# Eight weight groups prepared before the first tile: four staging buffers in turn, the low halves on VectorE alone

## The chip, the cores and the metric

The kernel runs on one core of a Trainium2 chip. The metric is the device time of one execution in microseconds (us), the median of three runs. The core has a matrix engine (TensorE, PE in the profile), VectorE (DVE), ScalarE (ACT), GpSimd (POOL), and queues that start transfers (SyncE, SP, here). Each engine works through its own list of instructions in order, and the engines wait for each other by semaphores that are written out by hand.

## The reference

One layer of a hybrid decoder over a prompt of 2048 tokens and 8 single new tokens, model width 1024, in fp32. What matters here:

```
u = rmsnorm(x, norm_in)
proj = u @ w_in                      # 1024 x 2832, split into nine parts
z = g_low @ w_gate_up + b_gate;  log_a = log_sigmoid(z) / 16
o_gla = gated linear attention(gq, gk, gv, log_a)       # 4 heads, recurrent state
o_swa = sliding-window attention(sq, sk, sv, sinks)     # 8 heads, window 128
h = x + concat(rmsnorm(o_gla) * silu(g_gate), o_swa * silu(s_gate)) @ w_out
y = rmsnorm(h, norm_f)
```

## The kernel before

Every product of an activation with a weight is made of fp16 matmuls: both factors are split into a high and a low half, and three matmuls (high by high, high by low, low by high) are added up in one PSUM bank. So the weights have to be split before anything can be multiplied by them, and they have to be scaled first so that the largest fits fp16.

**Preparing the weights.** The weights come in eight groups (`PREP`): group 0 is `sklow` (272 columns), 1 `gqk`, 2 `sq`, 3 `gv`, 4 `gg`, 5 `sg`, 6 and 7 the halves of the output projection (512 columns each). A group is 8 row blocks of 128 rows. For group i:

- `load_w(i)` (SP) brings it as fp32 into a staging buffer. There are four: two halves of the scratch tensor `flex`, and the room of `w_out_hi` and of `w_out_lo`, which are not in use yet. A buffer is loaded again when the group in it has been split.
- `sum_w(i)` (ACT) and `row_bound(i)` (DVE) bound the values in it, ACT over the last row blocks by summing, DVE over the first `SUM_ROWS` by a maximum. `row_bound` ends with a column `w_col`.
- `bound(i)` (PE) sums that column over the partitions with a matmul by ones (line 548), and `scale_w(i)` (DVE) makes the scale of it.
- `hi_w(i)` (ACT, line 1052, 8 instructions) writes the high half; `lo_w(i)` writes the low half, source times scale minus high half: DVE (line 1502) for row blocks 2 to 7, POOL (lines 1822 and 1825) for row blocks 0 and 1.

DVE's order in group i is: first half of `lo_w(i)`, `scale_w(i + 1)`, second half of `lo_w(i)`, `row_bound(i + 2)`. ACT's order is `hi_w(i)`, `sum_w(i + 2)`.

**Tiles.** The prompt is worked through in 16 tiles of 128 tokens, then the 8 new tokens. The projections of a tile (`proj`, units `sklow`, `gqk`, `sq`, `gv`, `gg`, `sg`) are made on PE one tile ahead, so that PE has work while the other engines do the attention of the current tile; those of tiles 0 and 1 lie beside the preparation. A unit of 512 columns is 24 matmuls of 512 columns, or 96 of 128. The results of the units pass through two PSUM banks in turn (`pj`, a `Ring`): the third unit from any unit waits until ACT or DVE has taken the first out (`take_qk`, `take_sq`, `take_gate` on ACT, `take_kv`, `take_gv` on DVE). Its list for the first tiles is bc0, sklow0, bc1, gqk0, sklow1, gqk1, sq0, sq1, gv0, gv1, gg0, sg0, gg1, sg1, where the digit is the tile.

**A tile.** In `body(t)` DVE takes the gate logits z (`take_z`), the maxima of the first two score banks (`row_max`) and the running sums of the decays (`sums`), then multiplies the transposed probabilities by a window mask (`take_pt`, line 1378), builds the factors of the linear attention (`factors`), assembles its scores, and ends with norms, scaling and residual. PE follows: `values` (line 611), `leaf_scores` (line 637), `level_scores` (line 651), `gla_out` (lines 671 and 675), `turn_out` (line 698), `out_proj`. Most of what a tile works on lies in `flex`, so in the room of two staging buffers.

## Time and profile before

| | us |
|---|---|
| median of 3 runs | 1002.18 (1001.75 to 1004.89) |
| the profiled execution | 1003.19 |
| its span, first to last instruction | 1001.0 |
| preparation and the middle of tile 0 | 0 to 119.4 |
| tile 0 ends on PE | 149.8 |
| one tile afterwards | 54.0 |
| last tile and the 8 new tokens | from about 930 |

PE is busy for 924.5 us (92% of the span), DVE for 665.4, ACT for 377.6, POOL for 100.9. The table is read so: from 119.4 us on PE goes from one piece of work to the next, tile after tile; the idle time of PE lies ahead of that and at the end.

### The profile page before, as it was taken

The page shows a single profiled execution, that of the slowest core. Times are in us where ns is not written, and L with a number is a line of the kernel's source. Part 1 is how long each engine was busy: PE and PEld are TensorE (multiplying, and loading weights), DVE is VectorE, ACT ScalarE, POOL GpSimd, SP SyncE. Part 2 cuts the span into 40 slices and gives each one's busy share as a digit, 9 for nine tenths or more (in the row PEclk, how much of TensorE's full clock was granted, in tenths as well). Part 3 has the DMA queues.
Part 4 walks back from the last instruction along what each step waited for, and adds up shares of the span by engine and source line. Part 5 has one row for each costly group of instructions (what it writes and reads, how often), then busy time and mean ns, then how long its engine had stood idle before and what let it go on. Part 6 is the DMA issues. An engine that isn't in the chain of part 4 may idle for free.

```text
span 1001.0 us, 22336 instructions
## 1 busy us (share of the span) xinstructions
PE 924.5 (92%) x8445; PEld 658.1 (66%) x8445; DVE 665.4 (66%) x1953; ACT 377.6 (38%) x1016; POOL 100.9 (10%) x125
## 2 busy tenths in 40 slices
PE   1598599999999999999999999999999999999977
PEld 1573458686767757585768666675758586866855
DVE  5888858575675748485757657574858585765573
ACT  4774434343324333333434232433333343424210
POOL 1453301010100101010101000010101010101000
PEclk9799599999999999999999999999999999998776
DMA  8621102020202001020202020110102020101220
GB/s 328 269 107 64 63 1 86 1 86 1 87 1 75 12 26 62 2 85 2 87 1 85 2 87 1 45 42 18 70 1 86 1 86 1 46 1 44 77 105 23
DMA packets 15238, 56.77 MB, mean 57 GB/s; under 512 B 3569, under 2 KB 5001, under 8 KB 13840
## 3 DMA queue, kind: packets, MB, share of 16 engines
q1 hardware_dynamic: 14832, 55.09, 14.8%
q8 instruction: 79, 1.29, 0.5%
q14 instruction: 39, 0.32, 0.1%
q10 hardware_dynamic: 288, 0.07, 0.0%
HBM read 44.36 MB, written 10.78 MB: 55 GB/s over the span
## 4 chain that ended last, share of the span: by engine, by line
PE 85%; DVE 12%; issue 2%; DMA 1%; ACT 0%; DVEq 0%; SPq 0%
PE bank L508 21%; PE bank L510 21%; PE bank L509 21%; PE bank L611 6%; PE bank L651 3%; DVE w_in_hi_lo L1502 2%; DVE w_abs L1472 2%; PE bank L588 2%; PE bank L698 2%; PE bank L600 1%; PE bank L675 1%; PE bank L671 1%; DVE flex L1378 1%; PE bank L625 1%; PE bank L637 1%
## 5 line engine op out<-in xcount | busy, mean ns | idle before, releaser
L508 PE MATMUL bank<-u_hi,w_in_hi_lo 128*128 128x128 f16 (+1 forms) x1288 | 210.1, 215 | 11.3 <-DVE w_in_hi_lo L1502 11.3
L510 PE MATMUL bank<-u_hi,w_in_hi_lo 128*128 128x128 f16 (+1 forms) x1288 | 209.9, 215 | 5.4 <-issue 5.4
L509 PE MATMUL bank<-u_lo,w_in_hi_lo 128*128 128x128 f16 (+1 forms) x1288 | 209.9, 215 | 0.0
L508 PE MATMUL bank<-w_in_hi_lo,u_hi 128*128 128x512 f16 (+3 forms) x528 | 177.8, 344 | 0.8 <-ACT win_q L951 0.5
L510 PE MATMUL bank<-w_in_hi_lo,u_lo 128*128 128x512 f16 (+3 forms) x528 | 177.6, 344 | 0.0
L509 PE MATMUL bank<-w_in_hi_lo,u_hi 128*128 128x512 f16 (+3 forms) x528 | 177.6, 344 | 0.0
L508 PEld LDWEIGHTS bank<-u_hi,w_in_hi_lo 128*128 128x128 f16 x1288 | 125.5, 100 | 24.3 <-DVE w_in_hi_lo L1502 11.4
L509 PEld LDWEIGHTS bank<-u_lo,w_in_hi_lo 128*128 128x128 f16 x1288 | 124.5, 99 | 0.1
L510 PEld LDWEIGHTS bank<-u_hi,w_in_hi_lo 128*128 128x128 f16 x1288 | 124.6, 99 | 0.0
L508 PE MATMUL bank<-w_out_hi,ogT_hi 128*128 128x512 f16 x256 | 98.0, 383 | 0.0
L509 PE MATMUL bank<-w_out_lo,ogT_hi 128*128 128x512 f16 x256 | 97.9, 382 | 0.0
L510 PE MATMUL bank<-w_out_hi,ogT_lo 128*128 128x512 f16 x256 | 97.8, 382 | 0.0
L611 PE MATMUL bank<-win_v,flex 128*128 128x64 f32 x512 | 69.8, 288 | 19.2 <-DVE flex L1378 19.2
L611 PEld LDWEIGHTS bank<-win_v,flex 128*128 128x128 f32 x512 | 67.5, 206 | 27.7 <-DVE flex L1378 23.6
L510 PEld LDWEIGHTS bank<-w_in_hi_lo,u_lo 128*128 128x128 f16 (+1 forms) x528 | 52.4, 99 | 46.7 <-issue 0.7
L508 PEld LDWEIGHTS bank<-w_in_hi_lo,u_hi 128*128 128x128 f16 (+1 forms) x528 | 52.4, 99 | 45.0 <-issue 4.8
L509 PEld LDWEIGHTS bank<-w_in_hi_lo,u_hi 128*128 128x128 f16 (+1 forms) x528 | 52.4, 99 | 39.6 <-issue 0.8
L1833 POOL TENSOR_TENSOR flex<-decay_sum_leaf 128x256 f32<-128x256 f32 x16 | 11.5, 718 | 594.4 <-DVE decay_sum_leaf L1273 594.4
L1226 DVE TENSOR_TENSOR xT<-xT,bank 128x1024 f32<-128x1024 f32 (+1 forms) x17 | 19.7, 1161 | 77.4 <-PE bank L518 77.4
L991 ACT ACTIVATE flex<-flex,win_stat 128x128 f32<-128x128 f32 x128 | 50.4, 394 | 31.4 <-DVE win_stat L1367 31.2
L1019 ACT CAST ogT_hi<-bank 128x512 f16<-128x512 f32 x32 | 17.3, 588 | 92.5 <-PE bank L698 92.5
L510 PEld LDWEIGHTS bank<-w_out_hi,ogT_lo 128*128 128x128 f16 x256 | 25.3, 99 | 30.8 <-issue 1.1
(252 smaller groups left out, 1636.9 us busy)
## 6 DMA issues: line engine op xcount, KB each, us to landing
xT<-in_xT SPq DMA_DIRECT2D x16, 512.0 KB, 4.5
x_rows<-in_xq SPq DMA_DIRECT2D x16, 512.0 KB
flex<-in_w SPq DMA_DIRECT2D x4, 2048.0 KB, 9.1
flex<-in_xq SPq DMA_DIRECT2D x16, 512.0 KB, 3.3
out_y<-flex SPq DMA_DIRECT2D x16, 512.0 KB, 2.6
w_out_hi<-in_w SPq DMA_DIRECT2D x2, 2048.0 KB, 8.6
w_out_lo<-in_w SPq DMA_DIRECT2D x1, 2048.0 KB, 14.6
flex<-in_w SPq DMA_DIRECT2D x1, 1088.0 KB, 7.4
```

Of the source, the lines that this page charges most:

```text
L508: nc.tensor.matmul(out, a_hi, b_hi, start=start and i == 0, stop=False)
L509: nc.tensor.matmul(out, a_hi, b_lo, start=False, stop=False)
L510: mm = nc.tensor.matmul(out, a_lo, b_hi, start=False, stop=stop and i == last)
L588: mm = nc.tensor.matmul(at_ring.bank(name, t)[:, i * 2 * P:(i + 1) * 2 * P], sq[r:r + HD, t.p, 2 * pair + i, :], kwin[r:r + HD, t.p, :], s ...
L611: mm = nc.tensor.matmul(accS[:, c:c + HD], PT[:, u % 2, i, kb, :], vwin[:, t.p, kb, h * HD:h * HD + HD], start=kb == 0, stop=kb == 1)
L651: mm = nc.tensor.matmul(bank[:, c:c + P], EX[:, l0 + l, f, :], QE[:, l0 + l, f].rearrange("p h c -> p (h c)"), start=True, stop=True)
L698: tp = nc.tensor.transpose(bank[:, k * P:k * P + n], gates[0:n, c:c + P], ident[0:n, 0:n])
L991: e = nc.scalar.activation(PR[:, u % 2, i, :], PR[:, u % 2, i, :], ACT.Exp, scale=-1.0, bias=wst[:, 0, k:k + 1], accum_out=wst[:, 1, k:k + 1])
L1019: nc.scalar.copy(ogT_hi[:, 4 * g:4 * g + 4, 0:n], bank[:, :, 0:n]).then_inc(act_o.sem, 1)
L1226: V.tensor_tensor(xT[:, :, 0:n], xT[:, :, 0:n], bcast(pj.bank("bc", t)[:, 0:n], 1, DT), ALU.mult).then_inc(pj.freed["dve"], 1)
L1472: V.tensor_reduce(wabs[:, s, 0:SUM_ROWS], staged(i)[:, 0:SUM_ROWS], AX.X, ALU.max, apply_absolute_value=True).then_inc(w_dve, 1)
L1502: lo = V.scalar_tensor_tensor(out=w_slice(PREP[i], w_lo, wo_lo)[:, d], in0=staged(i)[:, d], scalar=gs[:, i % 2, d:d + 1], in1=w_slice(PREP ...
```

## The change

Four things are changed, all of them ahead of tile 1; the loop over the later tiles and the ending keep their instructions.

- **Staging in turn.** Groups go to the four buffers in turn, beginning with `w_out_hi` and `w_out_lo`. SP starts groups 0, 1 and 2 at once, then the second tile's x, then group 3, the constants, and groups 4 to 7 in order.
- **GpSimd leaves the weights.** DVE makes all eight row blocks of the low half.
- **ScalarE sums four row blocks instead of three**, squares instead of absolute values, and DVE's maximum covers four instead of five. The bound is now a root of a sum of squares, rounded to a power of two by integer arithmetic on the exponent: `row_bound` has two more small instructions, `scale_w` works without a reciprocal.
- **Preparation first.** Before, tile 0's z, maxima and sums were taken ahead of the last group. Now they come after it. On PE the `bound` matmuls stand in other places between the projections, `gg` and `sg` of tile 0 are projected before the tile's work, and 18 of the 24 matmuls of tile 1's `gg` stand around `leaf_scores`.

```diff
-STAGE_OF = [0, 1, 2, 3, 0, 2, 1, 0]
-LOAD_ORDER = [0, 1, 2, 3, 4, 6, 5, 7]
-POOL_ROWS = 2
-SUM_ROWS = 5
+STAGE_OF = [2, 3, 1, 0, 2, 3, 1, 0]
+SUM_ROWS = 4
...
             load_w(1)
+            load_w(2)
             load_x(Tile(1))
-            for i in LOAD_ORDER[2:4]:
-                load_w(i)
+            load_w(3)
...
@@ PE, ahead of the tiles @@
             proj(Tile(1), "gqk")
+            proj(Tile(0), "sq")
             bound(4)
-            proj(Tile(0), "sq")
             proj(Tile(1), "sq")
+            proj(Tile(0), "gv")
             bound(5)
-            proj(Tile(0), "gv")
+            proj(Tile(1), "gv")
+            pe.wait_ge(init, 1)
+            turn_low(Tile(0))
             bound(6)
-            proj(Tile(1), "gv")
+            proj(Tile(0), "gg")
             bound(7)
-            pe.wait_ge(init, 1)
+            proj(Tile(0), "sg")
...
@@ PE, in body(t), where early is tile 0 @@
                 turn_probs(t, 3)
+                if early:
+                    proj(nxt, "gg", 3)
                 leaf_scores(t)
-                if not early:
+                if early:
+                    proj_rest(nxt, "gg", 3, 6)
+                else:
                     proj(nxt, "gv")
...
@@ ACT, sum_w @@
                 for d in range(SUM_ROWS, DT):
-                    a = nc.scalar.activation(unread[d - SUM_ROWS], src[:, d], ACT.Abs,
+                    a = nc.scalar.activation(unread[d - SUM_ROWS], src[:, d], ACT.Square,
                                              accum_out=wabs[:, i % 2, d:d + 1])
...
@@ ACT, body(t) @@
+                log_gate(t)
+                probs(t, 0)
+                probs(t, 1)
+                if early:
+                    act.wait_ge(w_lo_done, NG)
+                    take_gate(t, 0)
+                    take_gate(t, 1)
+                    nc.scalar.preload_act_table_set(LOG_EXP_SET)
+                else:
                     take_sq(nxt)
                 decays(t)
...
@@ DVE, row_bound and scale_w @@
+                V.scalar_tensor_tensor(out=wsq[:, s, 0:m], in0=wabs[:, s, 0:m], scalar=float(n), in1=wabs[:, s, 0:m],
+                                       op0=ALU.mult, op1=ALU.mult)
+                V.tensor_tensor(wsq[:, s, m:DT], wabs[:, s, m:DT], w_gain(PREP[i])[:, m:DT], ALU.mult
+                                ).then_inc(w_dve, 1)
...
-                V.reciprocal(wcol[:, 3:4], wcol[:, 2:3]).then_inc(w_dve, 1)
+                V.tensor_scalar(scale, half_exp, -EXP_ONE, 189 * EXP_ONE, ALU.mult, ALU.add)
+                V.tensor_scalar(unscale, half_exp, EXP_ONE, 65 * EXP_ONE, ALU.mult, ALU.add).then_inc(w_dve, 1)
...
@@ DVE, lo_w @@
-                for d in (range(POOL_ROWS, 4), range(4, DT))[half]:
+                for d in (range(4), range(4, DT))[half]:
...
@@ POOL @@
-            for i in range(NG - 1):
-                lo_w(i)
-            differences(Tile(0))
-            lo_w(NG - 1)
```

The order of the instructions shows two places on which the prediction speaks. First PE between the second `gqk` (128-column matmuls) and the second `gv` (512 columns). The rows with `w_col,ones` are `bound(4)` and `bound(5)`; of each projection only the first matmul stands, with its waits (`proj_freed_act`: until ACT has taken a result out of the bank). Before:

```order
L548 MATMUL bank<-w_col,ones 128x1 [waits w_row_bound_done]
L508 MATMUL bank<-u_hi,w_in_hi_lo 128x128 [waits proj_freed_dve,dve_norm,w_lo_pool,w_lo_done]
...
L508 MATMUL bank<-u_hi,w_in_hi_lo 128x128 [waits proj_freed_act,dve_norm,w_lo_pool,w_lo_done]
...
L548 MATMUL bank<-w_col,ones 128x1 [waits w_row_bound_done]
L508 MATMUL bank<-w_in_hi_lo,u_hi 128x512 [waits proj_freed_act,dve_norm,w_lo_pool,w_lo_done]
```

And of the changed kernel, from `sq` of tile 0 on:

```order
L504 MATMUL bank<-u_hi,w_in_hi_lo 128x128 [waits dve_norm,proj_freed_dve,w_lo_done]
...
L544 MATMUL bank<-w_col,ones 128x1 [waits w_row_bound_done]
L504 MATMUL bank<-u_hi,w_in_hi_lo 128x128 [waits dve_norm,proj_freed_act,w_lo_done]
...
L504 MATMUL bank<-w_in_hi_lo,u_hi 128x512 [waits dve_norm,proj_freed_act,w_lo_done]
...
L544 MATMUL bank<-w_col,ones 128x1 [waits w_row_bound_done]
L504 MATMUL bank<-w_in_hi_lo,u_hi 128x512 [waits dve_norm,proj_freed_act,w_lo_done]
```

`bound(4)` moved behind `sq` of tile 0, and `bound(5)` behind `gv` of tile 0, whose first matmul waits for a bank that ACT frees.

Second SP at the start. Before (`w_out_hi` here holds group 2, `w_out_lo` group 3):

```order
L438 DMA flex<-in_w 128x2176
L438 DMA flex<-in_w 128x4096
L422 DMA xT<-in_xT 128x1024
L427 DMA x_rows<-in_xq 128x1024
L438 DMA w_out_hi<-in_w 128x4096
L438 DMA w_out_lo<-in_w 128x4096
```

and in the changed kernel, where the first `flex` holds group 2 and the second group 3:

```order
L435 DMA w_out_hi<-in_w 128x2176
L435 DMA w_out_lo<-in_w 128x4096
L435 DMA flex<-in_w 128x4096
L420 DMA xT<-in_xT 128x1024
L425 DMA x_rows<-in_xq 128x1024
L435 DMA flex<-in_w 128x4096
```

Group 2 moved ahead of the second tile's x, whose load waits until the first tile's is used up.

## Rows read from the trace of the kernel before

**Rows 1.** The page: TensorE's granted clock in 40 slices of the span.

```profile
PEclk9799599999999999999999999999999999998776
```

**Rows 2.** Windows by stage: length, busy time (count) by engine, PEclk, DMA share, GB/s.

```profile
core 0: us, PE busy (x) PEld busy (x) DVE busy (x) ACT busy (x) POOL busy (x), PEclk, DMA share, GB/s
0.00:141.00 141.00, 90.59 (x769) 67.12 (x769) 111.34 (x232) 79.80 (x180) 47.06 (x34) 0.87 0.38 148
203.80:930.00 726.20, 713.97 (x6498) 502.46 (x6495) 475.18 (x1485) 265.22 (x748) 48.79 (x83) 1.00 0.11 39
```

**Rows 3.** Waits of PE, 0 to 130 us: total, times, longest.

```profile
PE bank L548 <- DVE w_col L1478: 16.3, 6, 4.4
PE bank L611 <- DVE flex L1378: 12.3, 2, 9.6
```

**Rows 4.** Timeline, SP and ACT: start, duration, what, idle before and its releaser.

```profile
15.33 0.43 SPq L438 DMA_DIRECT2D w_out_hi<-in_w  x1
15.81 3.39 ACT L1052 ACTIVATE w_in_hi_lo<-flex,w_scale 128x272 f16<-128x272 f32 x8
25.34 0.63 ACT L1040 ACTIVATE junk<-w_out_hi 128x512 bf16<-128x512 f32 x1 [5.11 <-DMA w_out_hi<-in_w]
48.85 5.01 ACT L1052 ACTIVATE w_in_hi_lo<-w_out_lo,w_scale 128x512 f16<-128x512 f32 x8
67.97 1.25 ACT L951 ACTIVATE win_q<-bank,inv_scale_q 128x512 f32<-128x512 f32 x2
```

**Rows 5.** Timeline, DVE and POOL where both work on a group.

```profile
54.70 2.13 POOL L1825 TENSOR_TENSOR w_in_hi_lo<-w_out_lo,w_in_hi_lo 128x1024 f16<-128x1024 f32 x1
54.88 1.97 DVE L1476 TENSOR_TENSOR w_abs<-w_abs,norm_in 128x8 f32<-128x8 f32 x1
63.87 3.65 POOL L1822 TENSOR_SCALAR flex<-flex,w_scale 128x512 f32<-128x512 f32 x2 [7.04 <-ACT w_in_hi_lo L1052]
64.69 1.40 DVE L1502 SCALAR_TENSOR_TENSOR w_in_hi_lo<-flex,w_scale,w_in_hi_lo 128x512 f16<-128x512 f32 x2
```

**Rows 6.** Timeline, DVE: the steps of a group, and marks in tile 0.

```profile
28.43 2.81 DVE L1472 TENSOR_REDUCE w_abs<-w_out_hi 128x5 f32<-128x2560 f32 x1
39.77 1.22 DVE L1232 TENSOR_TENSOR u_lo<-xT,u_hi 128x1024 f16<-128x1024 f32 x1
58.29 0.15 DVE L1485 TENSOR_SCALAR w_col<-bank 128x1 f32<-128x1 f32 x1
58.81 2.73 DVE L1502 SCALAR_TENSOR_TENSOR w_in_hi_lo<-w_out_lo,w_scale,w_in_hi_lo 128x512 f16<-128x512 f32 x4
61.46 2.81 DVE L1472 TENSOR_REDUCE w_abs<-w_out_hi 128x5 f32<-128x2560 f32 x1
86.92 0.15 DVE L1485 TENSOR_SCALAR w_col<-bank 128x1 f32<-128x1 f32 x1
94.80 0.61 DVE L1258 TENSOR_SCALAR flex<-bank,b_gate 128x128 f32<-128x128 f32 x2 [2.09 <-PE bank L625]
102.30 6.95 DVE L1502 SCALAR_TENSOR_TENSOR w_out_lo<-flex,w_scale,w_out_hi 128x512 f16<-128x512 f32 x6
110.36 1.22 DVE L1378 TENSOR_TENSOR flex<-bank,window_mask 128x512 f32<-128x512 f32 x2
134.90 0.88 DVE L1431 TENSOR_SCALAR flex<-flex,row_max 128x512 f32<-128x512 f32 x2
```

**Rows 7.** Windows at the edges of PE's pieces, columns as in the second group.

```profile
39.91:56.38 16.47, 16.47 (x242) 16.29 (x242) 16.28 (x24) 10.03 (x20) 10.99 (x6) 0.84 0.60 224
57.34:68.23 10.89, 10.89 (x196) 10.89 (x195) 8.65 (x15) 9.58 (x23) 4.28 (x3) 1.00 0.05 21
68.89:74.23 5.34, 5.34 (x24) 2.25 (x24) 5.34 (x6) 4.76 (x9) 2.62 (x3) 1.00 0.20 46
85.94:92.96 7.02, 7.02 (x26) 2.75 (x26) 6.74 (x11) 1.19 (x3) 4.82 (x3) 0.76 0.00 0
119.41:125.54 6.13, 6.13 (x35) 6.05 (x36) 2.66 (x10) 4.04 (x5) 1.04 (x1) 0.64 0.00 1
125.54:129.23 3.69, 3.69 (x23) 2.56 (x23) 2.58 (x7) 1.42 (x3) 0.00 (x0) 1.00 0.02 4
129.23:149.80 20.57, 20.57 (x108) 10.24 (x108) 10.22 (x27) 7.81 (x19) 0.00 (x0) 1.00 0.00 0
```

More of the change, by code:

```diff
@@ L436, in load_w @@
                     sp.wait_ge(w_lo_done, before[-1] + 1)
-                    sp.wait_ge(w_lo_pool, before[-1] + 1)
                 sp.dma_start(staged(i).rearrange("p d c -> p (d c)"), w_d[:, off:off + DT * n]
@@ L452, in _ @@
                 sp.dma_start(dst, src).then_inc(const_in, 16)
-            for i in LOAD_ORDER[4:]:
+            for i in range(4, NG):
                 load_w(i)
             sp.wait_ge(w_lo_done, NG)
-            sp.wait_ge(w_lo_pool, NG)
             sp.wait_ge(w_hi_done, 2 * NG)
@@ L807, in _ @@
             proj(Tile(0), "sklow")
+            bound(2)
             bc(Tile(1))
-            bound(2)
             proj(Tile(0), "gqk")
@@ L826, in body @@
                 early = t.static and t.off == 0
-                turn_low(t)
-                if early:
-                    proj(t, "gg")
-                    scores(t, 0)
-                    gate_up(t)
-                else:
-                    proj(nxt, "gqk")
-                    gate_up(t)
-                    scores(t, 0)
-                if early:
-                    proj(t, "sg")
-                else:
+                if not early:
+                    turn_low(t)
+                    proj(nxt, "gqk")
+                gate_up(t)
+                scores(t, 0)
+                if not early:
                     proj(nxt, "sq")
@@ L856, in body @@
                 turn_keys(t)
-                proj(nxt, "gg", 3)
+                if early:
+                    proj_rest(nxt, "gg", 6)
+                else:
+                    proj(nxt, "gg", 3)
                 gla_out(t)
                 state_update(t)
-                proj_rest(nxt, "gg", 3)
+                if not early:
+                    proj_rest(nxt, "gg", 3)
                 proj(nxt, "sg", 5)
@@ L1484, in scale_w @@
                 dve.wait_ge(w_bound, i + 1)
[L1485 removed]
+                half_exp, unscale, scale = (wcol[:, k:k + 1].bitcast(I32) for k in (1, 2, 3))
+                V.tensor_scalar(half_exp, accG[:, i:i + 1].bitcast(I32), 24, None, ALU.logical_shift_right
                                 ).then_inc(w_dve, 1)
[L1487 to L1489 removed]
+                dve.wait_ge(w_dve, 5 * i + 4)
+                V.tensor_scalar(scale, half_exp, -EXP_ONE, 189 * EXP_ONE, ALU.mult, ALU.add)
+                V.tensor_scalar(unscale, half_exp, EXP_ONE, 65 * EXP_ONE, ALU.mult, ALU.add).then_inc(w_dve, 1)
+                dve.wait_ge(w_dve, 5 * i + 5)
+                V.tensor_scalar(gs[:, i % 2, :], w_gain(g), wcol[:, 3:4], W_TOP, ALU.mult, ALU.mult
+                                ).then_inc(w_scaled, 1)
+                c = 1.0 / W_TOP / (U_SCALE if g < len(GROUPS) else 1.0)
                 V.tensor_scalar(inv[:, g:g + 1], wcol[:, 2:3], c, None, ALU.mult)
@@ L1676, in _ @@
             V.memset(ones[:, :], 1.0).then_inc(ones_set, 1)
+            V.memset(kwin[:, 0, 0:P], 0.0)
+            V.memset(vwin[:, 0, 0, :], 0.0)
+            V.memset(S_bd[:, :, :, :], 0.0)
             dve.wait_ge(first_in, 16 * 2)
@@ L1685, in _ @@
             for i in range(NG):
-                if i == NG - 1:
-                    dve.wait_ge(w_lo_done, i)
-                    dve.wait_ge(w_lo_pool, i)
-                    take_z(Tile(0))
-                    row_max(Tile(0), 0)
-                    row_max(Tile(0), 1)
-                    sums(Tile(0))
                 lo_w(i, 0)
@@ L1708, in _ @@
                     scale_u(Tile(1))
-                if i == 1:
+                if i == 3:
                     dve.wait_ge(const_in, 16 * 13)
                     V.tensor_scalar(s_sink[:, 1:2], s_sink[:, 0:1], -1.0, None, ALU.mult)
-                    V.tensor_scalar(nsink[:, :], sink[:, :], -1.0, None, ALU.mult)
-                    V.memset(kwin[:, 0, 0:P], 0.0)
-                    V.memset(vwin[:, 0, 0, :], 0.0)
-                    V.memset(S_bd[:, :, :, :], 0.0).then_inc(init, 1)
+                    V.tensor_scalar(nsink[:, :], sink[:, :], -1.0, None, ALU.mult).then_inc(init, 1)
+                if i == 4:
+                    take_gv(Tile(0))
                 if i == 5:
-                    take_gv(Tile(0))
-                if i == 6:
                     take_gv(Tile(1))
             dve.wait_ge(w_lo_done, NG)
-            dve.wait_ge(w_lo_pool, NG)
             V.memset(QE, 0.0).then_inc(init, 1)
@@ L1726, in body @@
                 early = t.static and t.off == 0
-                if not early:
-                    take_z(t)
-                    row_max(t, 0)
-                    row_max(t, 1)
-                    sums(t)
+                take_z(t)
+                row_max(t, 0)
+                row_max(t, 1)
+                sums(t)
                 take_pt(t, 0)
@@ L1815, in _ @@
             G = nc.gpsimd
-            def lo_w(i):
-                pool.wait_ge(w_hi_done, 2 * i + 1)
-                src = staged(i)
-                for d in range(POOL_ROWS):
-                    s = G.tensor_scalar(src[:, d], src[:, d], gs[:, i % 2, d:d + 1], None, ALU.mult)
-                s.then_inc(w_in_place, 1)
-                pool.wait_ge(w_in_place, i + 1)
-                G.tensor_tensor(w_slice(PREP[i], w_lo, wo_lo)[:, 0:POOL_ROWS], src[:, 0:POOL_ROWS],
-                                w_slice(PREP[i], w_hi, wo_hi)[:, 0:POOL_ROWS], ALU.subtract).then_inc(w_lo_pool, 1)
             def differences(t):
@@ L1844, in gates_over_sums @@
                 G.tensor_tensor(g, g, bcast(wst[:, 5, :], 2, HD), ALU.mult).then_inc(pool_w.sem, 1)
-            for i in range(NG - 1):
-                lo_w(i)
-            differences(Tile(0))
-            lo_w(NG - 1)
             def body(t):
-                if not (t.static and t.off == 0):
-                    differences(t)
+                differences(t)
                 gates_over_sums(t)
```

63 lines of the change are left out of this document (19 added, 44 removed).

## The prediction, made before the changed kernel had run

> **What bounds the kernel now.** I began with the page's clock row and the windows by stage. The clock is full in nearly every slice but the first five and the last four [rows 1]. In the stage from 203.8 to 930 us PE is busy for 713.97 of 726.20 us, DVE for 475.18 [rows 2]: the loop over the tiles is bound by PE. The change leaves its instructions alone, so it can move only the ramp, 0 to 141 us, where PE is busy for 90.59 us and DVE for 111.34. PE's waits there say for what: 16.3 us for `w_col`, and 12.3 us for the masked probabilities of tile 0, one of them 9.6 us [rows 3]. Both are DVE's. From 119.41 us, when `values` of heads 4 to 7 begins, PE is busy to the edge of every window [rows 7]. The question is when PE gets to that point, and how much work is left behind it.
>
> **The price of a group on DVE.** A bundle of four low-half instructions goes from 58.81 to 61.46, 2.65 us [rows 6]; two more per group cost 1.32. The maximum over five blocks takes 2.81 us [rows 6]; four blocks cost between 4/5 of it (2.25) and all of it; a part of an instruction is fixed, so I take 2.28, 0.53 saved. Two more small instructions in `row_bound`, and one independent one in `scale_w`: each lies between nothing and 0.2, by `scale_w`'s own, four of them in 58.81 - 58.29 = 0.52 [rows 6]. I take 0.28 and 0.10. Against that the stalls beside POOL go: POOL's TENSOR_TENSOR runs from 54.70 to 56.83, and DVE's 8-element instruction, begun inside it, needs 1.97 us, where its neighbours take some 0.2 [rows 5]: about 1.9 us a group. So 1.32 - 0.53 + 0.38 - 1.9, a gain of 0.7 us a group, 5 to 6 over the eight. A group now costs DVE 2.87 (`row_bound`) + 0.62 (`scale_w`) + 5.30 (`lo_w`) = 8.8 us.
>
> POOL's other form is not in that sum: DVE's two low-half instructions at 64.69 took their usual 1.40 us though POOL's TENSOR_SCALAR ran from 63.87 to 67.52 [rows 5]. [...]
>
> **The start.** Group 2 was issued at 15.33 and ACT waited 5.11 us for it, until 25.34 [rows 4]; the norm of tile 1's x stands behind it on ACT, and DVE's maximum of group 2 began at 28.43 [rows 6]. Now group 2 is issued with the first two. ACT does four sums of 0.62 instead of three, so `hi_w(0)` ends near 15.81 + 0.61 + 3.3 = 19.7 [rows 4]. Before, 1 MB of x and then its 2 MB came within 10.0 us; at that rate the 6 MB of x, groups 0, 1 and 2 are there near 20, and less late with no gap in between: I take 19; at worst it lands when it did. ACT then sums until 22.2, squares x until 23.4, and after 0.7 us of statistics and 0.8 on DVE the maximum begins at 24.8: 3.6 us earlier. From it, `row_bound` 2.87, `take_kv` 0.66 at 27.9 (it waits for `sklow`), the x product 1.2 behind `bc`, now queued behind `bound(2)`, to 29.9, then 2.65 + 0.67 + 2.65: `lo_w(1)` ends at 35.9 instead of 39.77 [rows 6], 3.9 us earlier.
>
> **Where it goes.** PE is next. `gqk` of tile 0, `sklow` and `gqk` of tile 1 took 16.47 us from that point, partly at half clock (0.84 on the mean) [rows 7]. PE still idles for some 7 us ahead of it, so I keep the 16.47: 36.0 to 52.5. `sq` of tile 0 (half of 10.89 [rows 7]) now stands ahead of `bound(4)`: 57.9. DVE, ready for `scale_w(4)` at 53.7, gets it at 58.2. Before it got it at 58.29 [rows 6]. The 3.9 us are gone, though PE has one unit more behind it.
>
> The next step is worse. `bound(5)` stands behind `gv` of tile 0, which needs the bank of `sq0`; ACT frees it after `hi_w(4)` and `sum_w(6)`. So 58.2 + 0.7 (`scale_w(4)` up to its signal), + 4.9 (`hi_w`, [rows 4]) + 2.46 (four sums) + 0.63 (half of 1.25, [rows 4]): `gv0` begins at 66.9. It takes 5.34 us at full clock [rows 7]; before, `gv1`, 24 matmuls behind an idle stretch of 3.9 us, took 7.02 at a mean clock of 0.76 [rows 7]. Here PE idles 3.5 us (`sq1` ends at 63.5). Ends 5.34 and 7.02, with 7.8 if the half clock held as long as it did behind 39.91; nearest is 7.02. So `scale_w(5)` is at 74.2 (72.5 at full clock), while DVE stood ready at 67. I count a new stall of 5 to 7 us in DVE.
>
> From there nothing else is late: two groups with a `take_gv` each, 2 x (8.8 + 0.66) = 18.9; then from `scale_w(7)` 0.62 + 3 x 2.65 and 1.1 for the wait and memset ahead of tile 0: `take_z` at 102.8. Before, from 86.92 (`scale_w(7)`) to 110.36 (`take_pt`) it took 23.44 us, with z, maxima and sums (94.80 to 102.30, 7.5 us) inside and 6.95 for the last six low-half instructions [rows 6]. Now 9.7 + 7.5 = 17.2: `take_pt` at 110.3 instead of 110.36. The same time. Moving z behind the last group costs nothing by itself, since DVE does the same work in either order; ACT's two gates and table loads (3.9 us) fit beside `sums` and `take_pt`, with 0.5 us to spare before `factors`.
>
> **Behind `take_pt`.** 18 matmuls of `gg1`, once behind `turn_keys`, now stand around `leaf_scores`. Before, `values` began 9.05 us behind `take_pt` (119.41 - 110.36) and PE had idled. Now PE has `values` of heads 0 to 3, two transposes (to +5.1), nine matmuls at half clock (0.427 each, 3.8), `leaf_scores` 1.1, nine more at full clock 1.95 (3.8 at half): +12 to +14. Then the levels 3.9 us at full clock instead of 6.13 [rows 7], six matmuls 1.3 and `gla_out` 1.9: +19.1. Before `gla_out` ended at 129.23, +18.9. A draw. From there PE had 20.57 us [rows 7]; 15 matmuls (3.2 us) of that are gone, but `turn_out` needs the scaled rows, half of them at 134.90 + 0.44, 6.1 us behind `gla_out` [rows 6]. So only the slack goes: PE would reach it at +3.8 and waits until +6.2, saving 20.57 - 19.9 = 0.7 us.
>
> **Sum.** `take_pt` -0.1, `gla_out` +0.2, end -0.7 and a rounding of the last terms: -0.8 us. Against the profiled execution (1003.19, of which 1001.0 is span) that is 1002.4; against the median, 1002.18, it is 1001.4. I predict 1001.4.
>
> **Rivals.**
> *A, the clock stays up* (chance 0.20). Ahead of `gv0` the idle stretch is a little shorter than the 3.9 us after which the clock fell; in full clock `gv0` ends 1.7 us earlier, and if `gqk0` warms up one matmul unit sooner another 1 to 2 us come. -2.5 to -5, median near 998.6. For it: the 0.7 us gaps in rows 7 cost no clock. Against: 3.5 is near 3.9.
> *B, DVE bound throughout* (0.03). Without either `bound` wait DVE would be at `scale_w(5)` at 61, 13 us earlier: 988. Against it: PE alone needs 36.0 + 16.47 + 10.89 + 5.34 = 68.7 to get there.
> *C, PE is cold where it was warm: slower* (0.13). The mechanism is the new idle stretch ahead of `turn_out`, 2.4 us, behind `gla_out`. If it drops the clock, the last `sg` matmuls and the output projection run up to 5 us at half speed, 2.5 us lost; with the second nine of `gg1` cold (1.9) and `gv0` at 7.8 (0.8) it gives -0.8 + 5.2 = +4.4, 1006.6. It decides from the length of idle at which the clock falls: the 3.9 us ahead of 85.08 were enough, 0.7 us ahead of 68.89 were not [rows 7].
> *D, x1 behind group 2* (0.07). If x of tile 1 lands late or group 2 lands at 25, the 3.6 us of the start are lost. `gqk0` starts at 39.6, everything follows: +2.8, 1005.0.
> Forecast: 0.57.
>
> A measurement of this kernel can tell about 0.3%, 3 us, from no change. Faster by more: most of A's upper half and B, and a tail of the forecast, 0.20. Slower: C and part of D, 0.14. Same 0.66. The range reaches from A's middle to the near side of C: 998 to 1005.5.
>
> **What would show it.** In the profile of the changed kernel: DVE's small instructions at some 0.2 us everywhere; no ACT wait for group 2; DVE's maximum of group 2 near 24.8 and `gqk0` near 36; `bound(4)` near 58 and DVE idle 4 us ahead of it; PE waiting for `win_q` ahead of `gv`, DVE idle for 5 us or more ahead of `scale_w(5)` near 73; `take_pt` near 110; a PE wait of 2 us ahead of `turn_out`; tile 0 ending near 149. I am wrong if `gv0` doesn't wait, if the granted clock in it or in the output projection of tile 0 is other than said, or if a later tile takes longer than before (726.2 us for the stage [rows 2], 54.0 each).

## The result, and the profile after

| | before | changed |
|---|---|---|
| median, us | 1003.08 (1001.75 to 1004.89, 6 runs) | 1008.21 (1007.05 to 1013.38, 6 runs) |
| ratio to before, 95% | | 1.0066 (1.0049 to 1.0083) |
| span of the profiled execution | 1001.0 | 1005.8 |
| first mark: first `values` of tile 1 | 164.48 | 164.38 |
| from there to the first `values` of tile 14 | 707.24 | 712.36 |
| the rest | 129.28 | 129.06 |

The changed kernel is 5 us slower. The prediction said 1001.4 (998.0 to 1005.5). The lower three rows split the span at two marks: the first matmuls of `values` in tile 1, where the loop over the tiles has just begun, and those in tile 14, the second tile behind the loop. The ramp came out the same, as forecast, but that the two marks lie within 0.1 us of each other is luck: in the kernels below whose ramp is that of the changed kernel the first mark lies between 162.4 and 164.7, and in those with the ramp of the kernel before between 162.9 and 164.5. The whole loss lies in the loop, which the forecast took as fixed.

Of the executions behind the numbers below, one of the kernel before (1583.92 us) and one of `after_pad128` (1211.95 us, at a mean granted clock of 0.741) were in a slow state; the ratios leave both out, and so does the median given for `after_pad128`.

**The ramp.** The windows by stage of the changed kernel, columns as in [rows 2]:

```profile
0.00:141.00 141.00, 93.27 (x769) 64.82 (x770) 106.06 (x272) 85.66 (x196) 3.74 (x10) 0.87 0.38 148
203.80:930.00 726.20, 712.24 (x6470) 503.07 (x6467) 472.05 (x1471) 263.30 (x739) 48.84 (x83) 0.99 0.11 39
```

VectorE has 5.3 us less to do in the ramp, GpSimd next to nothing. The timeline of ACT and DVE in the changed kernel, at the places forecast (start, duration, what, idle before and its releaser):

```profile
19.79 0.61 ACT L1039 ACTIVATE ogT_hi<-flex 128x512 bf16<-128x512 f32 x1
24.85 2.28 DVE L1462 TENSOR_REDUCE w_abs<-flex 128x4 f32<-128x2048 f32 x1
57.23 0.16 DVE L1480 TENSOR_SCALAR w_col<-bank 128x1 int32<-128x1 int32 x1 [4.21 <-PE bank L544]
73.25 0.16 DVE L1480 TENSOR_SCALAR w_col<-bank 128x1 int32<-128x1 int32 x1 [7.02 <-PE bank L544]
101.96 0.48 DVE L1248 TENSOR_SCALAR flex<-bank,b_gate 128x128 f32<-128x128 f32 x2
109.33 1.28 DVE L1368 TENSOR_TENSOR flex<-bank,window_mask 128x512 f32<-128x512 f32 x2
```

ACT no longer waits for group 2 (5.11 us in [rows 4]), and VectorE's maximum of it begins at 24.85 instead of 28.43 [rows 6]. Then both gains go where the prediction saw them go: VectorE idles 4.21 us for `bound(4)` and 7.02 us for `bound(5)`, and `take_pt` is at 109.33 instead of 110.36. Windows of the changed kernel at `gv` of tile 0, at the last nine `sg` matmuls of tile 0's pass, and from `gla_out` to the end of the tile:

```profile
66.07:73.10 7.03, 7.03 (x27) 3.04 (x28) 0.16 (x1) 0.47 (x1) 0.00 (x0) 0.76 0.13 54
135.34:139.12 3.78, 3.78 (x12) 1.40 (x10) 1.96 (x6) 3.11 (x6) 0.00 (x0) 0.55 0.00 0
128.12:149.70 21.58, 19.21 (x93) 9.11 (x93) 10.22 (x27) 7.93 (x19) 0.00 (x0) 0.92 0.00 0
```

`gv0` ran at a mean clock of 0.76 and took 7.03 us. Behind the new idle stretch ahead of `turn_out` (2.37 us) the clock was down for eight or nine matmuls: the window took 3.78 us at a mean clock of 0.55, so some 1.7 us more than the 2.1 (3.78 x 0.55) that it takes warm, at full clock. That is the first term of rival C, which had it at 2.5 us; its two others did not come (the second nine `gg` matmuls ran at full clock, 1.00 from 118.30 to 123.00 us, and `gv0` took 7.03 us and not 7.8).

**The loop.** Rows of PE's and DVE's waits from 150 to 910 us (total, times, longest), before:

```profile
PE bank L611 <- DVE flex L1378: 6.9, 14, 0.5
PE bank L510 <- issue: 5.4, 5, 1.2
```

and in the changed kernel:

```profile
PE bank L606 <- DVE flex L1368: 10.8, 14, 1.6
DVE flex L1251 <- issue: 3.8, 3, 1.4
PE bank L506 <- issue: 3.3, 5, 0.9
DVE flex L1251 <- DVE flex L1248: 1.7, 2, 0.9
```

The second and fourth rows are new. L1248 and L1251 are the two steps of `take_z`, and no work stands between them in the program. "issue" means that the engine waited for nothing that the profile shows. The loop makes six passes of two tiles each, and so jumps back from the end of its body to its first instruction, its head, five times. Five times, once for each jump, VectorE stood still in `take_z`. The place behind the first jump, before (VectorE's timeline):

```profile
265.03 0.61 DVE L1258 TENSOR_SCALAR flex<-bank,b_gate 128x128 f32<-128x128 f32 x2 [2.92 <-PE bank L625]
265.67 0.29 DVE L1261 TENSOR_SCALAR flex<-flex 128x256 f32<-128x256 f32 x1
```

and in the changed kernel, with PE's row of `values` that waits at the end of it:

```profile
264.34 0.61 DVE L1248 TENSOR_SCALAR flex<-bank,b_gate 128x128 f32<-128x128 f32 x2 [2.32 <-PE bank L620]
266.36 0.29 DVE L1251 TENSOR_SCALAR flex<-flex 128x256 f32<-128x256 f32 x1 [1.41 <-issue]
273.96 2.32 PE L606 MATMUL bank<-win_v,flex 128*128 128x64 f32 x15 [1.62 <-DVE flex L1368]
```

PE's idle 1.62 us there was 0.53 before, and it has a price of its own. The next windows, before and changed:

```profile
273.56:278.00 4.44, 4.44 (x61) 4.44 (x62) 4.33 (x21) 2.77 (x9) 0.00 (x0) 1.00 0.02 4
```

```profile
273.96:278.00 4.04, 4.04 (x33) 4.04 (x34) 3.94 (x20) 2.76 (x9) 0.00 (x0) 0.66 0.00 0
```

The granted clock was 0.66 on the mean here, and it fell again behind the last jump, at 713 us (0.77 over 4 us). Each of these two tiles took 55.47 us from its `values` to those of the next tile instead of 53.84. So the 5.12 us are: PE's waits for the probabilities +3.9 (10.8 - 6.9), cold matmuls, at half clock (0.50 from 275.30 to 278.60 us and from 715.60 to 718.90), +3.3 (2 x 1.63), PE's own idle behind the jump -2.1 (3.3 - 5.4). That sums to 5.1.

**What VectorE waits for.** The list of DMA queues has two rows of instruction packets (packets, MB, share). In the windows of 0.2 us in which they fall, q14 has one at 261.8, one at 264.4 and one at 268.6 in the changed kernel. The second:

```profile
q14 instruction: 1, 0.01, 18.0%
```

It is on its way when VectorE stops behind L1248, at 264.95. Its own time, 18.0% of 16 engines' 0.2 us, is 0.58 us, so it ends near 265.0, and VectorE goes on at 266.36, 1.3 us later; at the four other jumps it goes on 1.3 to 1.5 us behind the end of such a packet too. What fills that time no trace shows. A packet is 8 KB (0.32 MB in 39). This makes a fetch of VectorE's own instructions the suspect, and the experiments begin there. In the compiled programs VectorE's stream has 351 instructions in the loop, from number 295 before and from number 327 in the changed kernel: the rewritten ramp moved the loop by 32 instructions. PE's loop, 2014 long, begins at 1669 before and at 1657 after. The loops of ScalarE and GpSimd moved as well; the memsets of the experiments leave them where they are.

### The profile page after: what moved, and what is told of

It is laid out like the page before. It is cut to its first block, busy times and chain, and to the rows that moved or that the text cites. A ratio compares the mean times of both kernels' runs of the same rounds, so it can differ in the third digit from the quotient of the medians.

```text
span 1005.8 us, 22346 instructions
## 1 busy us (share of the span) xinstructions
PE 930.2 (92%) x8445; PEld 658.6 (65%) x8445; DVE 660.0 (66%) x1993; ACT 382.5 (38%) x1032; POOL 57.6 (6%) x101
## 4 chain that ended last, share of the span: by engine, by line
PE 85%; DVE 10%; issue 2%; ACT 1%; DMA 1%; SPq 0%; DVEq 0%
PE bank L504 21%; PE bank L506 21%; PE bank L505 21%; PE bank L606 6%; PE bank L646 3%; PE bank L693 2%; PE bank L583 2%; PE bank L595 1%; PE bank L670 1%; PE bank L666 1%; DMA w_out_lo<-in_w 1%; DVE w_in_hi_lo L1497 1%; PE bank L632 1%; DVE w_out_lo L1497 1%; PE bank L620 1%
## 5 line engine op out<-in xcount | busy, mean ns | idle before, releaser
L504 PE MATMUL bank<-w_in_hi_lo,u_hi 128*128 128x512 f16 (+3 forms) x528 | 180.0, 349 | 4.1 <-issue 4.1
L505 PE MATMUL bank<-w_in_hi_lo,u_hi 128*128 128x512 f16 (+3 forms) x528 | 179.5, 348 | 0.0
L996 ACT ACTIVATE win_stat<-win_stat 128x8 f32<-128x8 f32 x16 | 3.3, 208 | 110.7 <-DVE win_stat L1374 110.7
```

Of the source, the lines that this page charges most:

```text
L504: nc.tensor.matmul(out, a_hi, b_hi, start=start and i == 0, stop=False)
L505: nc.tensor.matmul(out, a_hi, b_lo, start=False, stop=False)
```

## The experiments

Each gives its own median, with that of the kernel before on the same chip in brackets. "Head" is the number of the first instruction of the loop in VectorE's stream. "Stall" adds up the idle time in `take_z` over the five jumps. "Loop" is the time from the first `values` of tile 1 to those of tile 14, in the profiled execution, and "first mark" is where it begins. With the loop, 39 or 40 packets on q14 mean five fetches for each jump (39 - 14 = 25 over five jumps); 14 or 15 mean none within the loop. Loop, stall and marks are those of one execution each.

| kernel | VectorE's head | q14 packets | stall in `take_z` | loop | first mark | median |
|---|---|---|---|---|---|---|
| before | 295 | 39 | 0 | 707.24 | 164.48 | 1003.08 |
| changed | 327 | 39 | 5.5 | 712.36 | 164.38 | 1008.21 |
| after_pad8 | 335 | 14 | 0 | 706.04 | 162.43 | 1001.91 (1003.88) |
| before_pad31 | 326 | 40 | 4.1 | 708.29 | 163.65 | 1006.30 (1003.88) |
| after_pad64 | 391 | 39 | 0 | 706.82 | 163.37 | 1002.66 (1003.25) |
| after_pad128 | 455 | 40 | 7.3 | 713.06 | 163.30 | 1007.92 (1003.25) |
| after_pad136 | 463 | 15 | 0 | 705.30 | 164.69 | 1002.12 (1003.05) |
| before_pad44 | 339 | 15 | 0 | 707.86 | 164.06 | 1002.81 (1003.05) |
| after_pad8_pe | 335 | 15 | 0 | 707.16 | 162.51 | 1003.08 (1003.17) |
| after_bounds | 327 | 39 | 3.7 | 710.47 | 156.00 | 998.41 (1003.88) |
| after_bounds_pad8 | 335 | 14 | 0 | 705.16 | 154.62 | 993.05 (1003.88) |
| after_flat | none | 29 | 0 | 700.73 | 163.84 | 996.71 (1003.25) |
| before_flat | none | 28 | 0 | 700.72 | 162.87 | 995.87 (1003.25) |
| bounds_flat | none | 29 | 0 | 700.72 | 154.62 | 987.34 (1003.05) |
| bounds_flat_gg | none | 29 | 0 | 700.70 | 160.11 | 992.20 (1003.05) |
| bounds_flat_gg9 | none | 29 | 0 | 700.71 | 154.79 | 987.68 (1003.17) |

### Moving VectorE's loop head

**after_pad8** and **before_pad31** put small instructions on VectorE ahead of everything, while it waits for the first transfers (before, its second instruction begins at 7.67 us; in `after_pad128` 60 of the memsets took 1.72 us). The tiles are untouched; `before_pad31` differs in 31 for 8 and starts from the kernel before.

```diff
             V.memset(ones[:, :], 1.0).then_inc(ones_set, 1)
+            for k in range(8):
+                V.memset(pad[:, k:k + 1], 0.0)
```

> The changed kernel with eight one-column memsets added at the start of VectorE's program, where VectorE is idle until 7.7 us. Nothing else changes, so the ramp should end where it does (tile 0 at 149.7 us). Theory F (instruction fetch behind the loop's back edge: the two instructions of take_z, L1248 and L1251, are torn apart by up to 1.4 us because a block of VectorE's program ends between them): moving the loop by eight instructions takes the edge of the block ahead of the loop's first instruction; the 'issue' idle time ahead of take_z's third instruction goes (3.8 us in 3 cases before), no stage of the loop has a clock under 1.00, and the time falls by 3 to 5 us, to 1003 to 1005. Rival P (the loop got slower since tile 0 leaves it in another state, by clock or by phase): the time stays at 1008.

> The kernel before, with 31 one-column memsets at the start of VectorE's program, where it is idle; by a count of rows and waits this sets its loop where that of the changed kernel stands. Theory F: the ramp is as before (tile 0 ends at 149.8 us), the idle time between take_z's instructions appears behind the back edges, and the kernel before gets slower by 2 to 5 us with no change of its work, to 1005 to 1008. If the count is off by a few instructions, the gap appears some instructions later, or not at all. Rival P: 1003 as before.

Eight idle instructions made the changed kernel 6 us faster by the medians: ratio to before 0.998 (0.9968 to 0.9991) instead of 1.0066. That is more than the 3 to 5 us expected. In the profiles the loop is 6.3 us shorter; the first mark comes 2.0 us earlier, since the clock stayed up in `gv0` (last section), and behind the loop 2.1 us are lost again. Its queue and wait rows:

```profile
q14 instruction: 14, 0.11, 0.0%
```

```profile
PE bank L607 <- DVE flex L1369: 6.9, 14, 0.5
PE bank L507 <- issue: 2.7, 5, 0.8
```

The fetches are gone, the stall is gone, and PE's wait is 6.9 us as before. In the other direction, 31 instructions brought the stall into the kernel before (ratio 1.0027, 1.0015 to 1.0039; median 1006.30, within the 1005 to 1008 expected):

```profile
PE bank L612 <- DVE flex L1379: 9.4, 14, 1.3
PE bank L511 <- issue: 3.8, 5, 0.9
DVE flex L1262 <- issue: 2.2, 2, 1.1
DVE flex L1262 <- DVE flex L1259: 1.9, 3, 0.8
```

Here the clock never fell in the loop, which lost 1.1 us: PE's waits for the probabilities +2.5 (9.4 - 6.9), its own idle behind the jump -1.6 (3.8 - 5.4). But the profiled execution was the fastest of ten. Seven of the others took 1005.6 to 1008.1 us, at mean granted clocks of 0.953 to 0.956, and the two others took 1003.3 and 1003.7, at 0.959 and 0.957; no trace shows where their clock was lost. So the same stall costs 1 to 5 us, and part of that is what the clock does with it. Why PE's own idle time fell here, with its head at 1669 as before, is not shown.

**after_pad64** and **after_pad128** ask whether it is the place or just some memsets: the same edit with 64 and 128.

> The changed kernel with 64 one-column memsets on VectorE near its beginning (59 ns each at most, while VectorE waits for the first transfers); the tiles are untouched. Measured from the first `values` after tile 0 to the last, the loop took 707.2 us before, 712.4 changed, 706.0 with 8 memsets, and its trace shows on queue q14, in packets of 8 KB (128 instructions of 64 bytes), 39 instruction packets before and changed, 14 with 8 memsets. Theory F (the place of the loop in VectorE's instruction stream decides, in blocks of 128): the loop, some 350 instructions long, lies over three blocks with 8 memsets and over four with 64. So q14 has some 39 packets again, but the loop's first block ends long behind take_z, as before, so that no stall stands between take_z's instructions: loop 706.5 to 708.5, median 1003 +-2. Rival G (extra instructions ahead of the loop shift the phase of the engines or of the clock, and any number of them helps): 14 packets or no relation, loop 706 as with 8. Rival H (blocks of 256, edge beyond +64): no fetches, 706.

The 64 bytes of an instruction can be estimated from the runs. The cost of the jump comes back after 128 memsets (below), and from none to 128, as from 8 to 136, q14 has one packet of 8 KB more (39 and 40, 14 and 15): 8192 / 128 = 64. A count of one packet is coarse, as 31 memsets brought one too. The other queue, q8, fits the same size. In `after_flat` it has 50 packets of 16 KB from 163.84 to 864.57 us, over thirteen tiles of 1007 instructions of PE (2014 / 2), or 62.6 bytes an instruction; 64 would be 51 packets:

```profile
q8 instruction: 50, 0.82, 0.5%
```

> As the last, with 128 memsets: one whole block. Theory F: the loop lies against the block edges just as in the changed kernel without memsets. q14 has 39 or 40 packets, VectorE stands for some 1.1 to 1.4 us between take_z's two forms behind back edges, loop 711 to 713, median 1008 +-2. Rival G: loop 706, median 1002. Rival H (blocks of 256): the edge is half a block away, no stall there, loop 706 to 708.

With 64 the fetches are back and hurt nobody in the profiled execution, which was the second fastest of ten; four of the others took 1004.5 to 1008.3 us, so the median's interval (ratio 1.0005, 0.9986 to 1.0025) leaves room for a small cost. With 128 everything is as with none, the stall larger still:

```profile
q14 instruction: 40, 0.33, 0.1%
```

```profile
PE bank L607 <- DVE flex L1369: 12.6, 14, 1.9
DVE flex L1252 <- issue: 7.3, 5, 1.7
PE bank L507 <- issue: 2.2, 5, 0.8
```

That rules out that any number of memsets helps, by the phase of the engines or of the clock (rival G), and blocks of 256 (rival H).

**after_pad136** and **before_pad44** are the cures one block further on, and for the kernel before.

> The changed kernel with 136 memsets, one block and 8. Theory F: as with 8, some 14 or 15 packets on q14 (one more block ahead of the loop), no stall in take_z, loop 706, median 1002 +-2. If more memsets only make things worse (128 gave 713): 712 or more, median 1008.

> The kernel before with 44 one-column memsets on VectorE near its beginning, which puts its loop where it lies in the changed kernel with some 4 to 13 memsets (the changed kernel has 40 instructions more ahead of the loop, or 31 with the separate waits counted). Theory F: the loop fits three blocks, q14 has some 14 instruction packets instead of 39, no fetch within the passes, loop from first to last `values` 706.0 instead of 707.2, median 1001.5 +-1.5. If memsets are no cure but only the changed kernel's ramp with 8 is: 39 packets and 707 to 708, as with 31 memsets.

`after_pad136` came out as said: 15 packets, 705.3 us. So heads 335 and 463 are free of fetches, 295, 326, 327, 391 and 455 are not: a period of 128, with an edge of a block between 327 and 335. A loop of 351 instructions that begins up to 33 behind an edge lies over three blocks (3 x 128 = 384), elsewhere over four; the packets fit three blocks that stay and four that don't. In `before_pad44` the fetches went too, but its loop stayed at 707.86: half of that expectation failed. VectorE had no stall to lose there, and what stands out in that loop is PE's own idle time behind the jump:

```profile
PE bank L511 <- issue: 5.5, 5, 1.2
```

**after_pad8_pe** moves PE's head instead, from 1657 to the 1669 of the kernel before.

```diff
                 pe.wait_ge(w_row, i + 1)
+                for k in range(3 if i == 0 else 0):
+                    nc.tensor.matmul(accG[:, i:i + 1], ones[:, :].broadcast_to([P, P]), wcol[:, 0:1],
+                                     start=True, stop=True)
```

> The changed kernel with the 8 memsets on VectorE, and on PE three more copies of the first `bound` matmul (each 4 instructions in the compiled program, the same value written again), so that PE's loop begins at instruction 1669 of its stream as in the kernel before, not at 1657. Theory F': what a back edge costs depends on where each engine's loop lies in its own stream; PE's idle time `<- issue` ahead of the first projection behind it was 5.4 us in all (5 times, longest 1.2) in both kernels with the head at 1669, whatever VectorE did, and 2.2 to 4.2 (longest 0.9) in those at 1657. So here 5 to 5.6, longest 1.2, no fetches of VectorE within the passes (14 packets), and a loop of 707.4 to 708.2, as the 707.9 of the kernel before with 44 memsets. Rival: PE's idle time there comes from other differences of the kernel before: 2.7, 706.0 as without the copies.

```profile
PE bank L507 <- issue: 4.9, 5, 1.2
```

PE's idle stretches of 1.2 us came back, behind three of the five jumps; the loop took 707.16 us, against 706.04 without the copies. That is in the direction of the expectation and a little short of it (707.4 to 708.2). Without a stall of VectorE's the loop took 705.16 to 706.82 us in the four profiles with PE's head at 1657, and 707.16 to 707.86 in the three with 1669. So PE's place seems to matter, by about 1 us over the loop, and the change then gained this microsecond, which hid a part of what VectorE lost. It is less certain than VectorE's part: each loop is one execution, the medians cannot show 1 us (ratios 0.998, 0.9968 to 0.9991, without the copies and 1.0001, 0.9986 to 1.0016, with them), and `before_pad31`, with its head at 1669, had 3.8 us of this idle time, longest 0.9.

### No loop at all

**after_flat** and **before_flat** write the twelve tiles of the loop out (the expectations speak of ten tiles in five passes; it is six passes and five jumps).

```diff
-            with eng.Fori(0, (NT - 4) // 2) as j:
-                body(Tile(1, j))
-                body(Tile(2, j))
-            for n in range(NT - 3, NT - 1):
+            for n in range(1, NT - 1):
                 body(Tile(n))
```

> The changed kernel without the loop: the ten tiles of its five passes are written out one behind the other, the same instructions in the same order on every engine. Theory F: nothing jumps back, the instructions come in order, and every tile takes the 53.84 us of the tiles without a back edge: from first to last `values` 13 x 53.84 = 699.9 us instead of 712.4, median near 1008.2 - 12.5 = 995.7 (994 to 998). Rival I (the later tiles are longer because the changed ramp leaves PE, the other engines or the clock in another phase, whatever the loop is): the loop keeps its 5 us on before's, 705 us, and after_flat is some 5 us slower than before_flat.

> The kernel before without the loop, in the same way. Theory F: 13 x 53.84 = 699.9 instead of 707.2, median near 1003 - 7.3 = 995.7 (994 to 998): the same as after_flat within 2 us, so that without the loop the change is worth about nothing, as its ramp shows. Rival I: 5 us less than after_flat.

The two loops differ by 0.01 us (700.73 and 700.72; 53.90 a tile), the medians by 0.8 us (996.71, 994.92 to 997.22; 995.87, 994.90 to 997.94), which is no difference. Without back edges, the jumps to the head, the change is worth nothing, and the forecast for the ramp was a gain of 0.8 us, too small to be measured. Instructions are still fetched (29 packets), now one block after the other, and nobody waits: PE's waits in `after_flat` from 150 to 910 us have no row for the projections behind "issue". The loop had cost 6.5 us before and 11.6 us after the change.

### The two `bound` matmuls

**after_bounds** puts them back where they stood, and **after_bounds_pad8** adds the 8 memsets.

```diff
-            proj(Tile(0), "sq")
             bound(4)
+            proj(Tile(0), "sq")
             proj(Tile(1), "sq")
-            proj(Tile(0), "gv")
             bound(5)
+            proj(Tile(0), "gv")
```

> The changed kernel with bound(4) put back ahead of sq of tile 0 and bound(5) back ahead of gv of tile 0. Worked out as in the prediction: scale_w(4) at 52.9 instead of 57.2, scale_w(5) at 62.7 instead of 73.25, gv of tile 0 without an idle gap ahead of it, take_pt of tile 0 at 100.6 instead of 109.5, and tile 0 ends 8 to 9 us earlier, at 141. The loop keeps its loss of about 5 us against before. So 999 to 1001. If the two waits were not what took back the gain of the leaner preparation, tile 0 ends at 149.7 as now and the time stays at 1008.

> Both edits together: bound(4) and bound(5) where they were before, and eight memsets ahead of the loop on VectorE. If both theories hold the gains add up: tile 0 ends at 141 us and the loop loses nothing against before, 994 to 996. Rival P: as the one with the bounds alone.

VectorE's `scale_w(4)` and `scale_w(5)` in `after_bounds`:

```profile
53.85 0.15 DVE L1480 TENSOR_SCALAR w_col<-bank 128x1 int32<-128x1 int32 x1
63.69 0.16 DVE L1480 TENSOR_SCALAR w_col<-bank 128x1 int32<-128x1 int32 x1 [0.85 <-PE bank L544]
```

Of the idle 4.21 and 7.02 us, 0 and 0.85 are left, and the first mark comes 8.4 us earlier. Ratios to before: 0.9946 (0.9927 to 0.9965), and with the memsets 0.9900 (0.9883 to 0.9916). Both medians lie somewhat below what was expected (998.41 for 999 to 1001, 993.05 for 994 to 996). The loop's loss stays in the first and goes in the second: two separate causes.

**bounds_flat** is `after_bounds` without the loop.

> The changed kernel with `bound(4)` and `bound(5)` back in front of `sq` and `gv` of tile 0, and with the tiles of the loop written out. The place of the two matmuls alone gave 8.4 us at the first `values` (164.4 to 156.0), the flat program gives 11.6 us on the loop (712.4 to 700.7). Theory F (two separate causes that add): median near 1008.2 - 9.8 - 11.5 = 987, range 985.5 to 989. If the ramp's gain came only together with some luck in PE's clock, it is 990 to 994.

987.34 us (986.90 to 988.64), ratio 0.9850 (0.9833 to 0.9867), as expected: the fastest kernel here, 15.7 us below the kernel before. 9.9 us of it are ramp (154.62 against 164.48) and 6.5 us loop.

### The matmuls of tile 1's `gg`

**bounds_flat_gg** takes the 18 matmuls away from around `leaf_scores`, and puts all 24 behind `turn_keys`. **bounds_flat_gg9** restores the order of the kernel before: 9 behind `turn_keys`, 15 behind `state_update`.

```diff
-                if early:
-                    proj(nxt, "gg", 3)
                 leaf_scores(t)
-                if early:
-                    proj_rest(nxt, "gg", 3, 6)
-                else:
+                if not early:
                     proj(nxt, "gv")
...
-                if early:
-                    proj_rest(nxt, "gg", 6)
-                else:
-                    proj(nxt, "gg", 3)
+                proj(nxt, "gg", 3)
                 gla_out(t)
                 state_update(t)
-                if not early:
-                    proj_rest(nxt, "gg", 3)
+                proj_rest(nxt, "gg", 3)
```

(the second; the first has `proj(nxt, "gg")` for tile 0 ahead of `gla_out`, and nothing behind `state_update`)

> As bounds_flat, with the 18 matmuls of tile 1's `gg` that stand around `leaf_scores` of tile 0 put back behind `turn_keys`. The prediction called this edit a draw: the levels wait on other engines whether or not PE is warm. So within 1 us of bounds_flat. Rival: the 18 matmuls fill an idle stretch of PE and keep its clock up; without them it is 2 to 4 us longer.

> bounds_flat with tile 1's `gg` exactly as in the kernel before: 9 of its 24 matmuls behind `turn_keys`, 15 behind `state_update` (the last kernel had all 24 behind `turn_keys`). The prediction called this edit a draw: then the first `values` after tile 0 lies within 1 us of bounds_flat's 154.6. From the traces: the levels again cold as in bounds_flat_gg, which put that mark at 160.1, but the 15 matmuls fill the 2.4 us ahead of `turn_out`: 157.5 to 158, median near 990.5. So the edit would be worth some 3 us here.

The windows from `values` of head 2 to the end of the levels, in `bounds_flat`:

```profile
111.17:114.96 3.79, 3.79 (x36) 3.78 (x35) 0.90 (x3) 0.00 (x0) 0.97 (x1) 1.00 0.00 0
```

and in `bounds_flat_gg9`:

```profile
109.11:115.66 6.55, 6.55 (x34) 6.54 (x35) 2.55 (x9) 0.21 (x1) 1.04 (x1) 0.57 0.00 0
```

The filling keeps PE's clock up and makes the levels 2.8 us shorter, but they begin 2.1 us later, and the 15 matmuls that are missing behind `gla_out` leave PE idle 2.4 us ahead of `turn_out`. Both kernels reach the first mark at the same time (154.62 and 154.79), with medians 0.3 us apart: the draw that the prediction had said, and not the 3 us that I expected of this run. `bounds_flat_gg` was 5 us slower (992.20), where I had expected at most 1, but it was no test of the draw: with all 24 ahead of `gla_out` nothing fills the stretch ahead of `turn_out` (2.36 us idle), and the levels are cold besides (a mean clock of 0.51 from 109.80 to 116.60 us). One of its four executions took 988.09 us, at a mean granted clock of 0.960 where the three others had 0.953, so part of its loss is the clock's.

## Why the prediction was wrong, by its own steps

- **What bounds the kernel: here it failed.** "The change leaves its instructions alone, so it can move only the ramp." The instructions are the same, but not their place in the stream. The loop took 5.1 us more: the term that the prediction put at nothing is VectorE's stall behind each of the five jumps, 5.5 us in all, for which PE waited 3.9 us more and lost 3.3 at half clock, less 2.1 of PE's own idle time. Moved 8 places further, VectorE's loop lost nothing. The prediction named the sign of its own failure ("if a later tile takes longer than before") without a rival for it. The rows that could have led there were in the profile before: tiles behind a jump took 54.9 to 55.6 us and the others 53.84, and PE's row with 5.4 us of "issue" said that a jump is not free. So it is not quite so either that all idle time of PE lies ahead of 119.4 us and at the end, as was said of the profile before: PE stood still for 12.2 us of the stage from 203.8 to 930 us (726.20 - 713.97).
- **The price of a group.** Right. The forecast was 8.8 us, and 9.46 with a `take_gv` (8.8 + 0.66): `scale_w(6)` and `scale_w(7)` are at 82.71 and 92.17, 9.46 apart. The maximum takes 2.28 us over four blocks and 2.81 over five; at the same 0.53 for every block 0.16 of it is fixed. The stalls beside POOL were there: two pairs of low-half instructions, at 33.35 and 75.45 us, with POOL's TENSOR_TENSOR beside them at 33.35 and 75.64, took 3.33 and 3.27 us where others took 1.40. Before, the longest single one took 2.67 us; in the changed kernel none took more than 0.76, and the 8-element instruction took 0.17 each time.
- **The start.** Right: 24.85 for the maximum (24.8 forecast), `gqk0` at 35.95 (36.0).
- **The two waits for `bound`.** Right in kind, each forecast 1 us late: 57.23 and 73.25 (58.2 and 74.2 forecast), 7.02 us of idle time where 5 to 7 were said. `after_bounds` shows them to be worth 8.4 us at the first mark. Rival B, "without either `bound` wait", put VectorE at `scale_w(5)` at 61; it was 63.69.
- **`gv0`'s clock.** Right in this execution, 7.03 us, but by luck. In four of the seven profiles with this ramp the same idle stretch went with the other outcome (last section), so the forecast had a coin in it, worth 1.7 us. Rival A turned on this coin; its 2.5 to 5 us needed more than it.
- **Behind `take_pt`.** `take_pt` at 109.33 instead of 110.3, `gla_out` ended 18.8 us behind it (19.1 forecast), PE waited 2.37 us for `turn_out` (2.4). The saving of 0.7 us at the end became a loss, since the last `sg` matmuls of tile 0's pass ran cold and took 1.7 us more. Tile 0 ended at 149.70, against 149.80.
- **The sum.** -0.8 us was forecast for the ramp; it was -0.1 at the first mark, and +0.8 between the medians of the two kernels without a loop, both within what the first mark varies between kernels with one ramp (about 2 us). The error of the whole is the term that was not there: +5.1 us.

## What to carry to other kernels

A loop's time was not a property of its body alone here: 707.24 and 712.36 us with the same instructions. Where a kernel has a hardware loop on several engines, count the instructions ahead of its head before and after a change, compare the iterations behind a jump with the others, and look for idle time behind "issue" and for the count of instruction packets; a few idle instructions ahead of the head, or writing the passes out, is a cheap test that tells a real gain from a moved head. Do this before judging any edit of the ramp, since 32 instructions of VectorE, which is not what bounds the loop, outweighed here all that the edit did to the ramp. And a small matmul on which another engine's chain hangs goes ahead of the long projections: the place of the two `bound` matmuls was worth 8.4 us.

## What the runs showed of the hardware

- VectorE fetches instructions in packets of 8 KB on q14, 128 of 64 bytes by the estimate at `after_pad64`: memsets on VectorE alone changed the count there from 39 to 14. The queue does not seem to be VectorE's alone: in `after_flat` its stream is 2280 instructions long, 18 packets of 128, and q14 has 29. The cost of a jump has a period of 128 instructions: loop of 706.0 us at +8, 706.8 at +64, 713.1 at +128, 705.3 at +136.
- Fetches alone cost nothing that could be measured: the kernel before has them, `before_pad44` has none, and their ratio is 0.9992 (0.9983 to 1.0002). What goes with the stall is how soon behind the head the next edge of a block comes: by the edge found above, 1 to 8 instructions on at head 327, where `take_z` stalls, 33 to 40 at 295 and 65 to 72 at 391, where it does not. The packet at 264.4 us has its like in the kernel before, at 264.8.
- PE has a cost behind the jump too, 2.2 to 5.5 us over the five in every kernel with a loop. Stretches of 1.2 us came only with its head at 1669, but not in `before_pad31`. Neither of the two places tried was free; only the written-out program was. That it is a fetch is not shown.
- PE's wait ahead of the first `values` behind a jump sometimes brought the granted clock down and sometimes did not, with no order by length: it fell behind waits of 1.62 and 1.37 us in the changed kernel (0.66 and 0.77 over the 4 us behind them), of 1.32 in `after_bounds` (0.69) and of 1.89 in `after_pad128`, and stayed full behind 1.38 in the changed kernel, 1.35 in `before_pad31` and 1.50 to 1.73 at the four other jumps of `after_pad128`. Behind the waits of some 0.5 us in the kernels without the stall it never fell.
- The same idle stretch can go either way. `gv0`, behind 3.50 us of idle, ran partly at half clock in the changed kernel (7.03 us, 0.76), in `after_pad136` and in `after_flat`, and at full clock in `after_pad64`, `after_pad128`, `after_pad8_pe` and `after_pad8`, here the last:

```profile
66.41:71.75 5.34, 5.34 (x27) 2.60 (x28) 0.16 (x1) 0.47 (x1) 0.00 (x0) 1.00 0.14 61
```

The idle time ahead does not decide the clock by itself. What does was not found out here.
